# Two-block transformer kernel: the split weight buffers placed 128 bytes further on

## The chip, the cores and the metric

The kernel runs on one NeuronCore of a Trainium2 chip. The metric is the time of one execution on the device, in microseconds (us); of several runs the median counts.

## The reference

The input is 256 tokens of 1024 features, with 16 meta tokens put ahead, so T = 272. Two layers of a first block follow, and then one layer of a second block with attention, a gated scan and a mixture of experts. In the first block all matrix products are of this kind:

```python
for l in range(DEPTH):                                  # DEPTH = 2
    h = h + 0.5 * swiglu(rmsnorm(h, ffn1_norm[l]), ffn1_w_gate[l], ffn1_w_up[l], ffn1_w_down[l])   # d_ff 2816
    proj = rmsnorm(h, mix_norm[l]) @ w_in[l]            # 1024 x 3584
    ...                                                 # retention and differential attention
    h = h + jnp.concatenate([y_ret, y_diff], axis=-1) @ w_out[l]
    h = h + 0.5 * swiglu(rmsnorm(h, ffn2_norm[l]), ffn2_w_gate[l], ffn2_w_up[l], ffn2_w_down[l])
```

All of it is float32.

## The kernel before, in words

Features lie on the 128 partitions and tokens along the free dimension; h is 8 chunks of 128 features by 272 tokens. Weights stream from memory into a ring of 7 slots of 8 KB per partition; the queue that starts these DMAs is SyncE's, in an order written out as a list (FILLS). The ring tensor has 12 slots' length: behind the seven slots come four buffers, w_split0 to w_split3, of 8 KB per partition each, and a last stretch for small things (rv, rstd, lam_prod, mod_sums, and later in the second block ctx_acc, ctx_sq, f2eps, last_sum, S_acc).

A product in float32 is made from three matmuls in the faster type float32r. Each half slot of weights (1024 floats per partition, eight blocks of 128 x 128) is split: ScalarE writes the rounded part w_hi into a w_split buffer (`weights_hi`, L1517), then VectorE writes the rest w_lo = w - w_hi behind it (`weights_lo`, L1987). The activations are split in the same way, into x_hi and x_lo for the products that read h, hid_hi and hid_lo for the down projections, y_hi and y_lo for the output projection of the mixer. TensorE then adds w_hi x_hi + w_hi x_lo + w_lo x_hi in PSUM:

```python
pe.matmul(to, w[:, 0, k], hi, start=first, stop=False)      # L754
pe.matmul(to, w[:, 0, k], lo, start=False, stop=False)      # L755
return pe.matmul(to, w[:, 1, k], hi, start=False, stop=last_)   # L756
```

In each, the block w[:, i, k] (128 floats, 512 bytes per partition) is loaded as weights and hi or lo (272 columns, or 256 where the meta tokens are no longer wanted) is streamed. Semaphores pass the buffers on: split_ready counts VectorE's halves, split_used TensorE's, and ScalarE may overwrite a buffer four halves later. `ffn` runs through 22 pairs of gate and up tiles (x) and then 22 blocks of the down projection (hid) for each of four feed-forward stages, `mixer` through 28 input tiles (x) and 8 output tiles (y) in each layer.

Where these operands lie matters for what follows. In the built program the ring begins at byte 16,512 of each partition and the arena, which holds the activations, at byte 114,816. x_hi and x_lo begin at arena + 4 x 2224 and then every 1280 bytes, that is at byte 123,712 and on; hid_hi and hid_lo at byte 168,000 and on, every 1280 bytes; y_hi at 167,936 and y_lo at 176,640, every 1088 bytes without a gap. With 256 columns the x and y operands are read from 64 bytes further on, and the hid operands from their start. w_split0 begins at ring + 7 x 8192 = 73,856. The output projection of the second block (L1303, L1308, L1309) has weight buffers of its own in the ring's range, at multiples of 4096 from the ring's start, and streams y2_lo and y2_hi in chunks of 1024 bytes from bytes 131,712 and 139,904, both of them 128 past a multiple of 256.

Of the kernel before, what the change touches and what calls it, by code (L numbers as in the profile page):

```python
# [12 lines left out]
P = 128  # L13
D = 1024
C = D // P
META, SEQ = 16, 256
T = META + SEQ
DEPTH = 2
# [9 lines left out]
SLOT = 2048  # L28
NS = 7
SPLITS = 4  # L30
# [4 lines left out]
MOD_COLS = SLOT // C  # L35
# [21 lines left out]
MOD_BUFFERS = 3  # L57
# [175 lines left out]
def build(nc, stream_ffn, stream_in, stream_out, stream_mod, stream_in2, stream_out2, stream_expert,  # L233
# [4 lines left out]
    with ExitStack() as ctx:  # L238
        def sb(name, shape, dt=fp32):
            return ctx.enter_context(nc.sbuf_tensor(name, shape, dt))  # L240
# [5 lines left out]
        ring = sb("ring", [P, 12 * SLOT])  # L246
        ring_at = nc.sbuf_base - 4 * 12 * SLOT
# [8 lines left out]
        def cut(tensor, at, *shape):  # L256

            n = int(np.prod(shape))
            piece = tensor[:, at:at + n]
            if len(shape) == 1:  # L260
                return piece
            names = "abcd"[:len(shape)]
            sizes = dict(zip(names[1:], shape[1:]))
            return piece.rearrange(f"p ({' '.join(names)}) -> p {' '.join(names)}", **sizes)

        def layout(tensor, at, items):

            found = {}
            for name, *shape in items:
                found[name] = cut(tensor, at, *shape)  # L270
                at += int(np.prod(shape))
            assert at <= tensor.shape[1], (at, tensor.shape)
            return found
# [12 lines left out]
        def parts(name, byte, *shape):  # L286

            n = int(np.prod(shape))
            return cut(nc.alloc_sbuf_tensor_at(name, [P, n], f32r, offset=byte), 0, *shape)
# [6 lines left out]
        def spaced(name, at, n):  # L296

            return [parts(f"{name}{c}", arena_at + 4 * (at + c * STEP), T) for c in range(n)]

        x_hi, x_lo = spaced("x_hi", C * T + LEAD, C), spaced("x_lo", C * T + LEAD + C * STEP, C)  # L300
        w_split = [parts(f"w_split{b}", ring_at + 4 * (NS + b) * SLOT, 2, C, P) for b in range(SPLITS)]
        X_AT = (NS + SPLITS) * SLOT
        m = layout(ring, X_AT, [("rv", 3, 512), ("rstd", T)])
        rv, rstd = m["rv"], m["rstd"]
        lam_prod = cut(ring, X_AT, DEPTH * 2, 64)

        hid = cut(arena, rest, F, T)
        gate_act = cut(con, CON["axial_cos"][0], 4, T)
# [5 lines left out]
        m = layout(arena, rest, [("tables", 4, T), ("cos", 2, T), ("swap", 2, T), ("vT", 2, T), ("e", 2, 2, T), ("rot", 8, T)])  # L314
# [6 lines left out]
        m = layout(arena, rest + 38 * T, [("dv", 3, 512), ("aT", 2, 3, P), ("first", 2, P), ("sT", DEC)])  # L321
# [4 lines left out]
        m = layout(small, 0, [("lam", DEPTH * 4), ("lam_dot", DEPTH * 2), ("neglam", DEPTH), ("sub", DEPTH)])  # L326
        lam_dot, neglam, sub_w = m["lam_dot"], m["neglam"], m["sub"]
        m = layout(small, 736, [("max", 2, 2), ("negmax", 2, 2), ("rsum", 2), ("nr", 2), ("sum", 9, 2), ("ss", 9), ("bn", 2, 6), ("mv", 9, 2),
                                ("dev", 18), ("ms", 2, META)])
# [26 lines left out]
        m = layout(arena, C * T, [("z", 4, KEYS), ("k", 4, KEYS), ("state", 4, 64), ("t1", 4, KEYS), ("B", 4, SEQ), ("G", 4, SEQ),  # L356
                                  ("q", 2, SEQ)])
# [4 lines left out]
        m = layout(arena, at_sq, [("zv", 4, SEQ), ("kdT", 8, P)])  # L362
        zv, kdT = m["zv"], m["kdT"]
        m = layout(arena, at_std, [("u", SEQ), ("s", SEQ), ("qx", 4, SEQ), ("vtok", 4, P)])
# [5 lines left out]
        m = layout(ring, NS * SLOT, [("qraw", 4, SEQ), ("qsin", 4, SEQ), ("qcos", 4, SEQ), ("qsq", 4, SEQ), ("kraw", KEYS), ("ksq", KEYS),  # L370
                                     ("kstd", KEYS), ("kcos", SEQ), ("ksin", SEQ), ("lev", 2, 4 * SEQ)])
# [3 lines left out]
        v_sq = q_sq.rearrange("p a b -> p (a b)")[:, 0:512].rearrange("p (h d) -> p h d", d=64)  # L375
        m = layout(ring, X_AT, [("S", 8, P), ("va", 2, SEQ), ("mix", 2, 2, P)])
        S_acc, mlp_v, mlp_mix = m["S"], m["va"], m["mix"]
        m = layout(ring, X_AT, [("acc", SEQ), ("one_sq", SEQ), ("f2", C, P)])
        ctx_acc, ctx_sq, f2eps = m["acc"], m["one_sq"], m["f2"]
        last_sum = cut(ring, X_AT + 2 * SEQ + C * P, SEQ)  # L380
        sh2b = cut(con, CON["ret_cos"][0], C, P)
        S_cross = cut(con, CON["ret_cos"][0], 2, 2, 2, P)
        m = layout(con, CON["decay"][0], [("wr", C, GROUPS + E), ("u", 2, SEQ), ("g", 2, SEQ)])
        w_r, mlp_u, hg = m["wr"], m["u"], m["g"]
        m = layout(arena, at_t1, [("oh", 2, SEQ), ("ohsq", 2, SEQ), ("ohstd", 2 * SEQ)])
# [11 lines left out]
        m = layout(arena, at_ex + 2 * D, [("xs", C, P), ("act", FE), ("hid", FE), ("hidT", 4, P), ("sel", 2, 2, CAP), ("selg", 2, 2, CAP),  # L397
                                          ("turned", SEQ), ("zeros", SEQ)])
# [7 lines left out]
        m = layout(arena, at_R, [  # L406
            ("lg", 2, GROUPS + E), ("gmax", 2), ("ngmax", 2), ("gsum", 2), ("gexp", 2, GROUPS), ("t4", 2, GROUPS),
            ("i4", 2), ("one4", 2, GROUPS), ("em", 2, GROUPS, PER_GROUP), ("m1", 2, GROUPS), ("m2", 2, GROUPS), ("dm", 2, GROUPS),
            ("t32", 2, GROUPS, PER_GROUP), ("i32", 2, GROUPS), ("allowed", 2, GROUPS, PER_GROUP), ("oh1", 2, E), ("oh2", 2, E),
            ("d", 2), ("ex", 2), ("g1", 2), ("g2", 2), ("gate", 2, E), ("chosen", 2, E), ("never", 2, E), ("total", E),  # L410
            ("rank", 2, E), ("most", 1), ("slot_gate", 1)])
# [9 lines left out]
        m = layout(more, 0, [("cr", SEQ), ("fa", C), ("f2", C), ("qstd", 16), ("rqs", 16), ("nrq", 16), ("amax", AHEAD, 2), ("anm", AHEAD, 2),  # L421
                             ("asum", AHEAD, 2), ("ars", AHEAD, 2), ("std3", 4), ("wr2", C, GROUPS + E), ("brow", GROUPS + E), ("zero", 80)])
        ctx_r, fa, f2, q_std, rqs, nrq = (m[x] for x in ("cr", "fa", "f2", "qstd", "rqs", "nrq"))
# [4 lines left out]
        m = layout(small, MOD_AT, [("mod", 48, 2), ("a1", C, 2), ("a2", C), ("cc", C, 2), ("unit", 64), ("ss", 8), ("vstd", 8), ("vr", 8),])  # L428
        mod_row = cut(arena, ARENA - P, P)
        mod, a1, a2, cc, unit_row, v_ss, v_std, v_rstd = (m[x] for x in ("mod", "a1", "a2", "cc", "unit", "ss", "vstd", "vr"))  # L430
        mod_product = cut(arena, hid_end, C, MOD_COLS)
        mod_sums = cut(ring, X_AT, MOD_BUFFERS, 2, MOD_COLS)
        assert hid_end + SLOT <= ARENA - P and MOD_BUFFERS * 2 * MOD_COLS <= 3 * 512
        SH1, SC1, G1, SH2, SC2, G2 = (slice(C * i, C * i + C) for i in range(6))

# [2574 lines left out]
```

## Time and profile before

| | us |
|---|---|
| median of 3 runs | 1729.33 (1729.3 to 1729.35) |
| the profiled execution, its own time | 1730.19 |
| its span, first to last instruction | 1728.6 |
| matmuls busy | 1700.6 |
| weight loads busy | 1394.3 |
| VectorE busy | 979.4 |
| ScalarE busy | 796.9 |
| GpSimd busy | 168.5 |

Matmuls overlap each other in the pipeline, so a matmul's duration in the profile is longer than the time that it adds; the step from the start of one to the start of the next is what it adds. Weight loads (PEld) run beside the matmul before them. The first block's work ends at about 1085 us; the experts fill the time from about 1270 us to the end.

### The profile page before, as it was taken

The page shows a single profiled execution, that of the slowest core. Times are in us where ns is not written, and L with a number is a line of the kernel's source. Part 1 is how long each engine was busy: PE and PEld are TensorE (multiplying, and loading weights), DVE is VectorE, ACT ScalarE, POOL GpSimd, SP SyncE. Part 2 cuts the span into 40 slices and gives each one's busy share as a digit, 9 for nine tenths or more (in the row PEclk, how much of TensorE's full clock was granted, in tenths as well). Part 3 has the DMA queues.
Part 4 walks back from the last instruction along what each step waited for, and adds up shares of the span by engine and source line. Part 5 has one row for each costly group of instructions (what it writes and reads, how often), then busy time and mean ns, then how long its engine had stood idle before and what let it go on. Part 6 is the DMA issues. An engine that isn't in the chain of part 4 may idle for free.

```text
span 1728.6 us, 30190 instructions
## 1 busy us (share of the span) xinstructions
PE 1700.6 (98%) x12315; PEld 1394.3 (81%) x12316; DVE 979.4 (57%) x1689; ACT 796.9 (46%) x1432; POOL 168.5 (10%) x173
## 2 busy tenths in 40 slices
PE   8999999999999999999999999999999999999998
PEld 7999988999999999998999999678764544445443
DVE  6776577678767777678778666476621111121111
ACT  6664455466656765665455445455621111111111
POOL 1000053210000100014413000101410000000000
PEclk9999999999999999999999999999999999999999
DMA  9555552254576577574245456032399999999997
GB/s 371 196 214 225 171 168 102 98 173 161 228 270 243 198 265 268 207 233 140 105 161 216 171 192 201 32 83 74 143 419 402 430 427 427 428 428 429 428 427 302
DMA packets 79107, 425.88 MB, mean 246 GB/s; under 512 B 16385, under 2 KB 33025, under 8 KB 42113
## 3 DMA queue, kind: packets, MB, share of 16 engines
q1 hardware_dynamic: 78400, 421.80, 63.2%
q8 instruction: 89, 1.46, 0.3%
q10 hardware_dynamic: 576, 2.29, 0.3%
q14 instruction: 42, 0.34, 0.1%
HBM read 423.02 MB, written 1.05 MB: 245 GB/s over the span
## 4 chain that ended last, share of the span: by engine, by line
PE 82%; DMA 6%; DVE 5%; ACT 4%; issue 1%; DVEq 1%; POOL 0%; POOLq 0%; SPq 0%; ACTq 0%
PE ps L754 16%; PE ps L755 16%; PE ps L756 16%; PE ps L1404 10%; DMA ring<-stream_expert 5%; PE ps L1455 5%; PE ps L1378 3%; PE ps L1083 2%; PE ps L1077 2%; DVE w_split L1987 2%; ACT w_split L1517 2%; PE ps L1089 2%; PE ps L1385 1%; PE ps L1386 1%; DVEq L2112 1%
## 5 line engine op out<-in xcount | busy, mean ns | idle before, releaser
L1987 DVE TENSOR_TENSOR w_split<-ring,w_split 128x1024 fp32r<-128x1024 f32 x335 | 421.7, 1279 | 239.5 <-ACT w_split L1517 238.9
L754 PE MATMUL ps<-x_hi,w_split 128*128 128x272 f32 (+1 forms) x1856 | 539.8, 291 | 6.5 <-DVE arena L2183 2.4
L755 PE MATMUL ps<-x_lo,w_split 128*128 128x272 f32 (+1 forms) x1856 | 530.9, 286 | 0.0
L756 PE MATMUL ps<-x_hi,w_split 128*128 128x272 f32 (+1 forms) x1856 | 530.8, 286 | 0.0
L1517 ACT ACTIVATE w_split<-ring 128x1024 fp32r<-128x1024 f32 x335 | 344.7, 1051 | 220.0 <-PE ps L756 218.6
L754 PEld LDWEIGHTS ps<-x_hi,w_split 128*128 128x128 f32 x1856 | 351.8, 190 | 14.6 <-issue 5.8
L755 PEld LDWEIGHTS ps<-x_lo,w_split 128*128 128x128 f32 x1856 | 351.9, 190 | 0.2
L756 PEld LDWEIGHTS ps<-x_hi,w_split 128*128 128x128 f32 x1856 | 351.7, 189 | 0.0
L754 PE MATMUL ps<-hid_hi,w_split 128*128 128x272 f32 (+1 forms) x704 | 200.0, 284 | 0.8 <-DVE arena L2106 0.8
L755 PE MATMUL ps<-hid_lo,w_split 128*128 128x272 f32 (+1 forms) x704 | 199.9, 284 | 0.0
L756 PE MATMUL ps<-hid_hi,w_split 128*128 128x272 f32 (+1 forms) x704 | 199.8, 284 | 0.0
L1404 PE MATMUL ps<-ring,arena 128*64 128x512 f32 x704 | 187.4, 594 | 3.8 <-DMA ring<-stream_expert 3.1
L1404 PEld LDWEIGHTS ps<-ring,arena 128*64 128x64 f32 x704 | 58.6, 137 | 99.5 <-issue 94.5
L2737 DVE TENSOR_TENSOR arena<-arena,ps 128x512 f32<-128x512 f32 x16 | 11.0, 688 | 217.6 <-PE ps L1404 217.6
L754 PEld LDWEIGHTS ps<-hid_hi,w_split 128*128 128x128 f32 x704 | 132.5, 188 | 1.1 <-DVE arena L2106 1.1
L755 PEld LDWEIGHTS ps<-hid_lo,w_split 128*128 128x128 f32 x704 | 132.5, 188 | 0.0
L756 PEld LDWEIGHTS ps<-hid_hi,w_split 128*128 128x128 f32 x704 | 132.5, 188 | 0.0
L1606 ACT ACTIVATE con<-con 128x272 f32<-128x272 f32 (+1 forms) x88 | 37.7, 428 | 157.1 <-DVE con L2104 156.2
L1914 ACT ACTIVATE arena<-ps,small 128x128 f32<-128x128 f32 x64 | 24.1, 456 | 163.3 <-PE ps L1378 163.3
L1594 ACT ACTIVATE ring<-ring,small 128x256 f32<-128x256 f32 x192 | 81.3, 494 | 0.0
L1455 PE MATMUL ps<-ring,arena 128*64 128x512 f32 x352 | 78.1, 595 | 0.0
L2748 DVE SCALAR_TENSOR_TENSOR ye_lo<-ps,arena,ye_hi 128x512 fp32r<-128x512 f32 x32 | 24.0, 751 | 91.5 <-ACT ye_hi L1930 76.6
(438 smaller groups left out, 2362.9 us busy)
## 6 DMA issues: line engine op xcount, KB each, us to landing
ring<-stream_ffn SPq DMA_DIRECT2D x131, 1024.0 KB, 4.9
ring<-stream_expert SPq DMA_DIRECT2D x48, 2048.0 KB, 24.9
ring<-stream_expert SPq DMA_DIRECT2D x36, 1024.0 KB, 12.4
arena<-stream_expert SPq DMA_DIRECT2D x16, 2048.0 KB, 25.4
ring<-stream_in SPq DMA_DIRECT2D x27, 1024.0 KB, 4.8
ring<-stream_mod SPq DMA_DIRECT2D x24, 1024.0 KB, 5.0
con<-stream_expert SPq DMA_DIRECT2D x8, 2048.0 KB, 26.1
ring<-stream_out SPq DMA_DIRECT2D x12, 1024.0 KB, 4.8
```

The source lines that it names most:

```text
L754: pe.matmul(to, w[:, 0, k], hi, start=first, stop=False)
L755: pe.matmul(to, w[:, 0, k], lo, start=False, stop=False)
L756: return pe.matmul(to, w[:, 1, k], hi, start=False, stop=last_)
L1077: last = pe.matmul(ps[:, b, 0:KEYS], w[:, c], x2n[:, :, c], start=c == 0, stop=c == C - 1)
L1083: last = pe.matmul(ps[:, b, i * SEQ:i * SEQ + SEQ], w[:, i, c], x2n[:, 0, c], start=c == 0, stop=c == C - 1)
L1378: last = pe.matmul(ps[:, 6 + half, (c % 4) * P:(c % 4) * P + P], h2t[:, t, c * P:c * P + P], sel[:, t], start=t == 0, stop=t == 1)
L1404: last = pe.matmul(ps[rows, 4 + part, 0:FE], xs[:, c, rows], w, start=c == 0, stop=c == C - 1)
L1455: last = pe.matmul(ps[rows, 6 + half, 0:512], hidT[:, f, rows], w[:, half * 512:half * 512 + 512], start=f == 0, stop=f == FE // P - 1)
L1517: nc.scalar.activation(w_split[n % SPLITS][:, 0], half_of(n), ACT.Copy).then_inc(hi_ready, 1)
L1594: last = nc.scalar.activation(to[:, c], w[:, c], ACT.Identity, scale=cc[:, c, v:v + 1])
L1606: nc.scalar.activation(gate_act[:, j % 4, t:T], gate_act[:, j % 4, t:T], ACT.Silu).then_inc(gate_act_ready, 1)
L1987: nc.vector.tensor_tensor(w[:, 1], half_of(n), w[:, 0].bitcast(fp32), ALU.subtract).then_inc(split_ready, 1)
```

## The change

The four w_split buffers begin 32 floats (128 bytes) further on, and so do most of the things that lie behind them. Nothing else is touched: the ring's slots, the activations, and every instruction, wait and DMA stay.

```diff
-        w_split = [parts(f"w_split{b}", ring_at + 4 * (NS + b) * SLOT, 2, C, P) for b in range(SPLITS)]
+        W_AT = NS * SLOT + 32
+        w_split = [parts(f"w_split{b}", ring_at + 4 * (W_AT + b * SLOT), 2, C, P) for b in range(SPLITS)]
         X_AT = (NS + SPLITS) * SLOT
-        m = layout(ring, X_AT, [("rv", 3, 512), ("rstd", T)])
+        FIRST_X = X_AT + 32
+        m = layout(ring, FIRST_X, [("rv", 3, 512), ("rstd", T)])
         rv, rstd = m["rv"], m["rstd"]
-        lam_prod = cut(ring, X_AT, DEPTH * 2, 64)
+        lam_prod = cut(ring, FIRST_X, DEPTH * 2, 64)
...
-        m = layout(ring, X_AT, [("acc", SEQ), ("one_sq", SEQ), ("f2", C, P)])
+        m = layout(ring, FIRST_X, [("acc", SEQ), ("one_sq", SEQ), ("f2", C, P)])
         ctx_acc, ctx_sq, f2eps = m["acc"], m["one_sq"], m["f2"]
-        last_sum = cut(ring, X_AT + 2 * SEQ + C * P, SEQ)
+        last_sum = cut(ring, FIRST_X + 2 * SEQ + C * P, SEQ)
...
-        mod_sums = cut(ring, X_AT, MOD_BUFFERS, 2, MOD_COLS)
+        mod_sums = cut(ring, FIRST_X, MOD_BUFFERS, 2, MOD_COLS)
```

## Rows read from the trace of the kernel before

**Rows 1.** The page's sections 1 and 4, and the granted clock by core.
```profile
PE 1700.6 (98%) x12315; PEld 1394.3 (81%) x12316; DVE 979.4 (57%) x1689; ACT 796.9 (46%) x1432; POOL 168.5 (10%) x173
...
PE ps L754 16%; PE ps L755 16%; PE ps L756 16%; PE ps L1404 10%; DMA ring<-stream_expert 5%; PE ps L1455 5%; PE ps L1378 3%; PE ps L1083 2%; PE ps L1077 2%; DVE w_split L1987 2%; ACT w_split L1517 2%; PE ps L1089 2%; PE ps L1385 1%; PE ps L1386 1%; DVEq L2112 1%
...
core 0: 1728.6 us, clock 0.998
```

**Rows 2.** Groups of TensorE by form: count | busy us, mean ns | idle before.
```profile
L754 PE MATMUL ps<-x_hi,w_split 128*128 128x272 f32 x1416 | 413.8, 292 | 6.1 <-DVE arena L2183 2.4 <-DVE x_lo L1992 2.2 <-DVE w_split L1987 1.4
...
L754 PE MATMUL ps<-hid_hi,w_split 128*128 128x272 f32 x528 | 151.4, 287 | 0.8 <-DVE arena L2106 0.8
...
L754 PE MATMUL ps<-x_hi,w_split 128*128 128x256 f32 x440 | 126.0, 286 | 0.4 <-ACT more L1602 0.2
...
L754 PE MATMUL ps<-hid_hi,w_split 128*128 128x256 f32 x176 | 48.6, 276 | 0.0
```

**Rows 3.** Timeline of TensorE, first and last of four stretches: start, duration, instruction.
```profile
574.84 0.29 PE L756 MATMUL ps<-x_hi,w_split 128*128 128x272 f32 x1
...
586.92 0.29 PE L755 MATMUL ps<-x_lo,w_split 128*128 128x272 f32 x1
...
699.78 0.29 PE L755 MATMUL ps<-hid_lo,w_split 128*128 128x272 f32 x1
...
711.99 0.28 PE L755 MATMUL ps<-hid_lo,w_split 128*128 128x272 f32 x1
...
914.80 0.28 PE L754 MATMUL ps<-x_hi,w_split 128*128 128x256 f32 x1
...
926.92 0.28 PE L756 MATMUL ps<-x_hi,w_split 128*128 128x256 f32 x1
...
1039.79 0.28 PE L754 MATMUL ps<-hid_hi,w_split 128*128 128x256 f32 x1
...
1051.91 0.28 PE L756 MATMUL ps<-hid_hi,w_split 128*128 128x256 f32 x1
```

**Rows 4.** Timeline, output projection of the second block: two rows, 22 steps apart.
```profile
1250.61 0.28 PE L1309 MATMUL ps<-y_lo,o_hi 128*128 128x256 f32 x1
...
1253.25 0.28 PE L1303 MATMUL ps<-y_hi,o_lo 128*128 128x256 f32 x1
```

**Rows 5.** Timeline, projection of y, one output tile: L754 of each chunk.
```profile
351.38 0.29 PE L754 MATMUL ps<-y_hi,w_split 128*128 128x272 f32 x1
...
351.76 0.29 PE L754 MATMUL ps<-y_hi,w_split 128*128 128x272 f32 x1
...
352.14 0.29 PE L754 MATMUL ps<-y_hi,w_split 128*128 128x272 f32 x1
...
352.52 0.29 PE L754 MATMUL ps<-y_hi,w_split 128*128 128x272 f32 x1
...
352.90 0.29 PE L754 MATMUL ps<-y_hi,w_split 128*128 128x272 f32 x1
...
353.28 0.29 PE L754 MATMUL ps<-y_hi,w_split 128*128 128x272 f32 x1
...
353.65 0.29 PE L754 MATMUL ps<-y_hi,w_split 128*128 128x272 f32 x1
...
354.04 0.29 PE L754 MATMUL ps<-y_hi,w_split 128*128 128x272 f32 x1
...
354.41 0.29 PE L754 MATMUL ps<-y_hi,w_split 128*128 128x272 f32 x1
```

**Rows 6.** Timeline, projection of y with 256 columns, 86 steps apart.
```profile
884.75 0.28 PE L755 MATMUL ps<-y_lo,w_split 128*128 128x256 f32 x1
...
894.89 0.28 PE L754 MATMUL ps<-y_hi,w_split 128*128 128x256 f32 x1
```

**Rows 7.** The filling instructions by line: count, duration ns min/median/max, starts, form.
```profile
L1987 DVE TENSOR_TENSOR w_split<-ring,w_split x335: 1211/1226/1814, 12.9 to 1075.5; 128x1024 fp32r<-128x1024 f32 x168
...
L1517 ACT ACTIVATE w_split<-ring x335: 1038/1047/1064, 11.8 to 1074.4; 128x1024 fp32r<-128x1024 f32 x168
```

## The prediction

> **What bounds the kernel now.** I read the page first: TensorE's matmuls are busy for 1700.6 us of a span of 1728.6 us [rows 1], so only something that shortens or lengthens the row of matmuls itself can move the time much. The chain that ended last says the same, and says where: the three lines of the split product (L754, L755, L756) hold 48% of the span, while the two instructions that fill the moved buffers (L1987 on VectorE, L1517 on ScalarE) hold 2% each [rows 1]. The groups by form then give the number of these products: 1416 x 3 = 4248 matmuls of 272 columns on x, 528 x 3 = 1584 of 272 columns on hid, 440 x 3 = 1320 of 256 columns on x and 176 x 3 = 528 of 256 columns on hid [rows 2] (of each three rows the first stands there); the rest, 384, work on y. The granted clock is 0.998 over the span [rows 1], that is, the upper level of 2.4 GHz, so the clock is not what limits them.
>
> The duration of one matmul (286 ns) is not what one costs, since they overlap. What one costs is the step from start to start, and I took it from the timeline, from the first and last of about a hundred in a stretch without a gap:
> - x, 272 columns: (586.92 - 574.84) / 98 = 123.3 ns [rows 3]
> - hid, 272 columns: (711.99 - 699.78) / 99 = 123.3 ns [rows 3]
> - x, 256 columns: (926.92 - 914.80) / 101 = 120.0 ns [rows 3]
> - hid, 256 columns: (1051.91 - 1039.79) / 107 = 113.3 ns [rows 3]
>
> The reader is to see the last two: same instruction form, same engine, same clock, same weight buffers, and 6.7 ns apart. Even the best is above its columns (256 / 2.4 = 106.7 ns; 272 / 2.4 = 113.3 ns). What differs between the two is where the operand that streams lies. So place in memory has a price in this kernel, and a change of place can be worth something in either direction. 7680 matmuls lie in these four groups, 0.45 ns on each of them is 3.5 us, or 0.2%.
>
> **The addresses.** From the layout in the code, with the ring at byte 16,512: a weight block begins at 73,856 + 512 i, which is 128 past a multiple of 256; after the change at 73,984 + 512 i. That is a multiple of 256, and by my sum 256 past a multiple of 512, not on one. Whether the period that matters is 256 or 512 the trace has to say; I will call the byte modulo 256 the phase. x_hi and x_lo have phase 64 for 272 columns and 128 for 256 columns (they start 16 floats later), hid_hi and hid_lo always 64. I call "distance" the phase of the streamed operand less that of the weights. Before: x and hid at 272 columns 192, x at 256 columns 0, hid at 256 columns 192. After, each less 128: 64, 128 and 64. The output projection of the second block has both operands at phase 128, thus distance 0 with other buffers, and its step is (1253.25 - 1250.61) / 22 = 120.0 ns [rows 4], the same as x at 256 columns: that speaks for the distance (or the pair of phases) as what sets the step.
>
> The best witness for the distances that come is the projection of y: its chunks are 1088 bytes long, so the eight chunks go through all four phases under an unchanged weight phase. In the order c = 4, 5, 6, 7, 0, 1, 2, 3 the starts of L754 are 0.38, 0.38, 0.38, 0.38, 0.38, 0.37, 0.39 and 0.37 us apart [rows 5]. By distance that is, per matmul: 128 (c = 4, 0) 126.7 ns; 192 (c = 5, 1) 125.0 ns; 0 (c = 6, 2) 128.3 ns; 64 (c = 7, 3) 125.0 ns. The rows are rounded to 0.01 us, so each of these is good to some 1.5 ns. Two distances that differ by 128 cost the same within that, and the odd ones cost less than the even ones. The change adds exactly 128. The witness has a weakness: its phases change every three matmuls, and it does not settle. At distance 192 it gives 125.0 ns where the steady stream gives 123.3, and with 256 columns its mean is (894.89 - 884.75) / 86 = 117.9 ns [rows 6], between the steady 120.0 and 113.3.
>
> **The change, part by part.**
> 1. x and hid at 272 columns, 5832 matmuls, distance 192 to 64. Not shown steady. Lower bound: the best step per column in the trace, 113.3 / 256 x 272 = 120.4 ns, so -2.9 x 5832 = -17 us. Upper bound: the worst of the y rows, 128.3 ns, so +5.0 x 5832 = +29 us. The nearest row is y's at distance 64, which equals y's at 192; I take 0.
> 2. x at 256 columns, 1320 matmuls, distance 0 to 128. Lower bound: 113.3 ns, -6.7 x 1320 = -8.8 us. Upper bound: above 120.0 no steady row of this width lies; y's difference of 192 to 0 (3.3 ns) once more on top would be +4.4 us. I take the mean of y at this width, 117.9: -2.1 x 1320 = -2.8 us.
> 3. hid at 256 columns, 528 matmuls, distance 192 to 64. From 0 (stays at 113.3) to +6.7 x 528 = +3.5 us (goes to 120.0). I take the same 117.9: +4.6 x 528 = +2.4 us.
> 4. y, 384 matmuls: the same four distances, dealt to other chunks: 0, within 384 x 1 ns = 0.4 us.
> 5. L1517 and L1987, 335 each. They write the moved buffer, and L1987 reads it beside the ring, which does not move. L1517 takes 1047 ns (1038 to 1064), L1987 1226 ns with a longest of 1814 ns [rows 7]. That two VectorE instructions of one shape differ so shows that something can hold them up, but TensorE's idle time before the 272-column products of x that ends on L1987 is 1.4 us in all [rows 2], and their cover is the ring of four buffers. If the cover went, it would be the 4% of the span that the chain gives them: 5% more on each is 0.04 x 1728.6 x 0.05 = 3.5 us. Only a longer run of such stalls counts. I take 0.
> 6. The things behind the buffers (rv, rstd, the context sums, f2eps, mod_sums) move by the same 128 bytes. They hold no instruction of the chain's larger lines; no instruction, wait or DMA is added or removed anywhere, the DMAs write the ring's seven slots, which stay, and the queues keep their order. 0.
>
> Sum: 0 - 2.8 + 2.4 + 0 = -0.4 us against the profiled execution's 1730.19 us (span 1728.6 us). The median of the runs is 1729.33 us, 0.86 us below the profiled one, and the forecast is made against it: 1729.33 - 0.4 = 1729 us, no change that this kernel's measurement tells (0.2% is 3.5 us).
>
> The Trainium skill speaks to this on its page "TensorE: Matmul & The Clock Gate", in "Step-by-step: what each phase is for": TensorE has two independent read ports, and loading the next weights takes no bandwidth from the running matmul. By that rule no distance could matter and the time stays; by the rows above a distance matters by up to 6.7 ns, so the measurement decides, and the rule adds no weight to the forecast. The page's isolated gap ("Back-to-back issue gap", columns / 2.4 + 2.5 ns) would be 115.8 and 109.2 ns; the trace has 123.3, 120.0 and 113.3.
>
> **The rivals.**
> - Faster, x at 256 columns leaves its bad place. Distance 0 is the one case where both operands start in the same phase, and it is the slowest steady row. If 128 is as good as 192: 113.3 ns, -8.8 us, 1720.5 us. For it: the 6.7 ns are there. Against: y at distance 128 (126.7) is nearer to 0 (128.3) than to 192 (125.0).
> - Faster, all 272-column products gain. If what costs is that a weight block lies 128 off its natural border, and not the distance, then 5832 matmuls come down towards 120.4 ns: 1729.3 - 17 = 1712 us, half of it 1721 us. Against: hid at 256 columns runs at 113.3 with the weights where they are.
> - Slower, the other side: distance 64 is a worse steady place than 192 for 272 columns. It decides from 0.6 ns per matmul on (0.6 x 5832 = 3.5 us). At y's 125.0 ns it is +1.7 x 5832 = +10 us, 1739 us; at 128.3 it is 1758 us. For it: 123.3 is already below every y row, so the present place may be a lucky one that the move loses. Against: y's equal 125.0 at 192 and 64.
> - Slower, hid at 256 columns alone loses its 113.3: +3.5 us, 1732.8 us, on the border of what can be told.
> - The change does nothing, since the cost repeats every 128 bytes, or since no phase of the weights matters: 1729.3 us. It cannot be told from the forecast by the time, only by the steps; it shares the forecast's chance. By my address sum the blocks reach a multiple of 256 only, so if what counts were the border of 512, the change would also miss it.
>
> **How the numbers follow.** Chances: no change (forecast and "does nothing") 0.38; x at 256 columns gains 0.23; all 272 columns gain 0.13; 272 columns lose 0.17; hid at 256 alone loses 0.06; VectorE and ScalarE slow down so that it shows 0.03. Faster by over 0.2%: 0.23 + 0.13 = 0.36. Slower: 0.17 + half of 0.06 + 0.03 = 0.23. Within: 0.38 + half of 0.06 = 0.41. The likeliest case's own range is 1726 to 1733 us. For 8 in 10, the range goes down past the x case (1720.5) to 1718 and up to y's 125.0 (1739); outside lie most of the 272-column gain and the deep end of the loss.
>
> **What would show it.** The steps from start to start in the same four stretches: I expect 123 to 124 ns at 272 columns for x and hid, 113 to 120 for x at 256 columns and 113 to 120 for hid at 256. In y's rows the pairs should change places by chunk and the mean stay at 126 and 118 ns. L1987 and L1517 should keep 1226 and 1047 ns. I am wrong if the steady step at 272 columns moves by more than 0.6 ns, in whichever direction; that one number decides.

## The result, and the profile after

The changed kernel takes 1745.03 us in the median of 4 runs (1744.63 to 1745.87), before 1729.34 us (1729.3 to 1733.19). The ratio is 1.009, with a 95% interval of 1.0078 to 1.0101: slower by 15.7 us. The profiled execution took 1744.85 us, with a span of 1743.2 us, 14.6 us more than before.

The page of the changed kernel, its sections 1 and 4 (all line numbers are two higher than before):

```profile
PE 1717.2 (99%) x12315; PEld 1411.1 (81%) x12316; DVE 978.1 (56%) x1689; ACT 797.9 (46%) x1432; POOL 169.4 (10%) x173
...
PE 88%; DMA 6%; DVE 3%; ACT 2%; issue 1%; DVEq 0%; SPq 0%; POOL 0%; POOLq 0%; ACTq 0%
PE ps L756 18%; PE ps L758 18%; PE ps L757 18%; PE ps L1406 10%; DMA ring<-stream_expert 5%; PE ps L1457 5%; PE ps L1380 3%; PE ps L1085 2%; PE ps L1079 2%; PE ps L1091 2%; DVE w_split L1989 1%; ACT w_split L1519 1%; PE ps L1387 1%; PE ps L1388 1%; PE ps L934 0%
```

Matmuls are busy for 1717.2 us, 16.6 us more, and the number of instructions is the same [rows 1]. The chain now has the three product lines at 54% where they had 48%, and the two filling lines L1989 and L1519 have fallen from 2% to 1% each; all of VectorE and ScalarE hold 3% and 2% of it, where they held 5% and 4%. So the loss is in TensorE's own row, and the waits for the other engines became smaller.

The timeline of the changed kernel in the four kinds of stretch that the prediction used, first and last matmul of each:

```profile
579.75 0.29 PE L757 MATMUL ps<-x_lo,w_split 128*128 128x272 f32 x1
...
591.91 0.29 PE L757 MATMUL ps<-x_lo,w_split 128*128 128x272 f32 x1
...
709.77 0.29 PE L758 MATMUL ps<-hid_hi,w_split 128*128 128x272 f32 x1
...
721.93 0.29 PE L758 MATMUL ps<-hid_hi,w_split 128*128 128x272 f32 x1
...
929.78 0.28 PE L758 MATMUL ps<-x_hi,w_split 128*128 128x256 f32 x1
...
941.88 0.28 PE L758 MATMUL ps<-x_hi,w_split 128*128 128x256 f32 x1
...
1049.77 0.28 PE L757 MATMUL ps<-hid_lo,w_split 128*128 128x256 f32 x1
...
1061.90 0.28 PE L758 MATMUL ps<-hid_hi,w_split 128*128 128x256 f32 x1
```

From start to start that is (591.91 - 579.75) / 96 = 126.7 ns for x and (721.93 - 709.77) / 96 = 126.7 ns for hid at 272 columns, where it was 123.3 [rows 3]; (941.88 - 929.78) / 102 = 118.6 ns for x at 256 columns (120.0 before); and (1061.90 - 1049.77) / 103 = 117.8 ns for hid at 256 columns (113.3 before). The sum over the matmuls: 3.4 x 5832 = 19.8 us, -1.4 x 1320 = -1.8 us, 4.5 x 528 = 2.4 us, together 20.4 us. The span grew by 14.6 us, so 5.8 us of this did not reach the time.

Both traces, read whole, say where it went. From the first to the last start of each group, with the waits in it, the time grew by 9.4 us for x and 4.2 us for hid at 272 columns and by 2.3 us for hid at 256. It fell by 1.4 us for x at 256 and stayed for y. Together this is 14.4 us.

- Waits, 3.9 us. From 20 us on, steps of 140 ns and more from one product to the next, with whatever lies between, were 174 before, 110.4 us in all, and 165 after, 105.4 us; the nine that went cost 1.1 us as ordinary steps. This is no accident of one trace: the two experiments below with the distances of the changed kernel show 105.4 us each, and the six that keep those of the kernel before in most of their rows show 108.9 to 111.0 us (the one that adds instructions left out). It fits with a slower TensorE that finds its operands ready more often.
- The start, 0.9 us. Between 9 and 12 us and between 12 and 14 us, among the first products and their waits, the granted clock was 0.72 and 0.57 in the trace before, and 1.00 in the one after. An experiment with the changed kernel's distances has slow steps there too, so this does not come from the change.
- The last 1 us is the rounding of the steps, and the mixers' rows at 272 columns, which do not settle and moved by less than 3.4 ns.

The groups by form of the changed kernel show one place where a wait went:

```profile
L756 PE MATMUL ps<-x_hi,w_split 128*128 128x272 f32 x1416 | 415.9, 294 | 6.3 <-DVE arena L2185 2.2 <-DVE x_lo L1994 1.9 <-DVE w_split L1989 1.9
...
L756 PE MATMUL ps<-hid_hi,w_split 128*128 128x272 f32 x528 | 152.6, 289 | 0.0
```

The idle time ahead of hid's products, 0.8 us before [rows 2], is gone. Ahead of x's it is the same. What this view calls idle is only a part; steps that stretch while the engine still counts as busy are the rest.

The instructions that fill the moved buffers, by line, and one stretch of y in the changed kernel:

```profile
L1989 DVE TENSOR_TENSOR w_split<-ring,w_split x335: 1211/1225/1795, 12.5 to 1089.9; 128x1024 fp32r<-128x1024 f32 x168
...
L1519 ACT ACTIVATE w_split<-ring x335: 1039/1056/1065, 11.5 to 1088.8; 128x1024 fp32r<-128x1024 f32 x168
```

```profile
349.71 0.29 PE L757 MATMUL ps<-y_lo,w_split 128*128 128x272 f32 x1
...
360.93 0.29 PE L756 MATMUL ps<-y_hi,w_split 128*128 128x272 f32 x1
```

L1989 has 1225 ns in the median and L1519 1056 ns, against 1226 and 1047 [rows 7]. The 9 ns of L1519 are not the price of the place: with the weights moved and the row at its old pace (the first experiment below) it takes 1048 ns, and with the weights where they were and the row slow (the second) 1057 ns. The mean step of y is (360.93 - 349.71) / 89 = 126.1 ns, as before.

### The profile page after: what moved, and what is told of

It is laid out like the page before. It is cut to its first block, busy times and chain, and to the rows that moved or that the text cites. A ratio compares the mean times of both kernels' runs of the same rounds, so it can differ in the third digit from the quotient of the medians.

```text
span 1743.2 us, 30190 instructions
## 1 busy us (share of the span) xinstructions
PE 1717.2 (99%) x12315; PEld 1411.1 (81%) x12316; DVE 978.1 (56%) x1689; ACT 797.9 (46%) x1432; POOL 169.4 (10%) x173
## 4 chain that ended last, share of the span: by engine, by line
PE 88%; DMA 6%; DVE 3%; ACT 2%; issue 1%; DVEq 0%; SPq 0%; POOL 0%; POOLq 0%; ACTq 0%
PE ps L756 18%; PE ps L758 18%; PE ps L757 18%; PE ps L1406 10%; DMA ring<-stream_expert 5%; PE ps L1457 5%; PE ps L1380 3%; PE ps L1085 2%; PE ps L1079 2%; PE ps L1091 2%; DVE w_split L1989 1%; ACT w_split L1519 1%; PE ps L1387 1%; PE ps L1388 1%; PE ps L934 0%
## 5 line engine op out<-in xcount | busy, mean ns | idle before, releaser
L1989 DVE TENSOR_TENSOR w_split<-ring,w_split 128x1024 fp32r<-128x1024 f32 x335 | 420.7, 1275 | 254.8 <-ACT w_split L1519 254.4
L1519 ACT ACTIVATE w_split<-ring 128x1024 fp32r<-128x1024 f32 x335 | 345.6, 1052 | 240.5 <-PE ps L758 238.5
```

What stands on the lines that cost most here:

```text
L1519: nc.scalar.activation(w_split[n % SPLITS][:, 0], half_of(n), ACT.Copy).then_inc(hi_ready, 1)
L1989: nc.vector.tensor_tensor(w[:, 1], half_of(n), w[:, 0].bitcast(fp32), ALU.subtract).then_inc(split_ready, 1)
```

## The experiments

Everything below is read in the same way: the step from start to start in a stretch of about a hundred matmuls. The kernel before ran beside the experiments on the same chips, at 1729.77 us in the median for the first four, 1729.64 us for the next four and 1729.5 us for the last three. Five of the kernels ran once only (the two shifts of the weights, the small things, the two sweeps); their steps carry the argument. Distances are in bytes modulo 256, streamed operand less weights.

**Is it the distance, or the place of the weights?** Two kernels make a square of the two. In the first, weights and operands both move (LEAD was 48):

```diff
-        w_split = [parts(f"w_split{b}", ring_at + 4 * (NS + b) * SLOT, 2, C, P) for b in range(SPLITS)]
+        W_AT = NS * SLOT + 32
+        w_split = [parts(f"w_split{b}", ring_at + 4 * (W_AT + b * SLOT), 2, C, P) for b in range(SPLITS)]
...
-        x_hi, x_lo = spaced("x_hi", C * T + LEAD, C), spaced("x_lo", C * T + LEAD + C * STEP, C)
+        X_LEAD = 16
+        x_hi, x_lo = spaced("x_hi", C * T + X_LEAD, C), spaced("x_lo", C * T + X_LEAD + C * STEP, C)
...
+        H_AT = hid_at + 32
```

> The weight buffers lie 128 bytes further on, as in the change, and x and hid lie 128 bytes further on too (for x the start is 128 bytes back, which is the same phase modulo 256). So the weights have phase 0 and the distances are those of the kernel before: 192 at 272 columns, 0 for x at 256, 192 for hid at 256. Theory of the distance: steps of 123.3, 120.0 and 113.3 ns and 1729 us (within 3 us; y keeps the changed distances). Theory of the weights' own phase: 126.7, 118.7 and 117.8 ns as in the changed kernel, and 1745 us.

1729.55 us, ratio to before 0.9999 (0.999 to 1.0009). Its timeline, three of the stretches (x at 272, x at 256, hid at 256):

```profile
579.83 0.28 PE L759 MATMUL ps<-x_lo,w_split 128*128 128x272 f32 x1
...
591.91 0.28 PE L758 MATMUL ps<-x_hi,w_split 128*128 128x272 f32 x1
...
929.74 0.28 PE L760 MATMUL ps<-x_hi,w_split 128*128 128x256 f32 x1
...
941.98 0.28 PE L760 MATMUL ps<-x_hi,w_split 128*128 128x256 f32 x1
...
1049.75 0.28 PE L759 MATMUL ps<-hid_lo,w_split 128*128 128x256 f32 x1
...
1061.99 0.28 PE L759 MATMUL ps<-hid_lo,w_split 128*128 128x256 f32 x1
```

12.08 / 98 = 123.3 ns, 12.24 / 102 = 120.0 ns, 12.24 / 108 = 113.3 ns. The weights lie where the change put them, and the loss is gone.

The mirror leaves the weights and moves x and hid alone (the last two edits of the diff above without the first).

> The mirror: the weight buffers stay where they were (phase 128), and x and hid move by 128 modulo 256. The distances are those of the changed kernel: 64, 128, 64. Theory of the distance: steps of 126.7 (272 columns), 118.7 (x, 256) and 117.8 ns (hid, 256), and 1744 to 1745 us. Theory of the weights' own phase: 123.3, 120.0 and 113.3 ns, and 1729 us. If only x's and hid's own phase counts, the result is a third set, equal to that of the kernel with both moved.

1745.55 us, ratio 1.0092 (1.0075 to 1.0109). Its timeline, x at 272 and hid at 256 columns:

```profile
579.82 0.29 PE L757 MATMUL ps<-x_lo,w_split 128*128 128x272 f32 x1
...
591.98 0.29 PE L757 MATMUL ps<-x_lo,w_split 128*128 128x272 f32 x1
...
1049.81 0.28 PE L757 MATMUL ps<-hid_lo,w_split 128*128 128x256 f32 x1
...
1061.94 0.28 PE L758 MATMUL ps<-hid_hi,w_split 128*128 128x256 f32 x1
```

12.16 / 96 = 126.7 ns and 12.13 / 103 = 117.8 ns: the whole loss, with the weights untouched. The weights' own place has no price; their distance to the streamed operand has. One number missed the expectation, x at 256 columns:

```profile
929.72 0.28 PE L757 MATMUL ps<-x_lo,w_split 128*128 128x256 f32 x1
...
941.96 0.28 PE L757 MATMUL ps<-x_lo,w_split 128*128 128x256 f32 x1
```

12.24 / 102 = 120.0 ns where 118.7 was expected. The row was at 118.6 ns before an interruption near 922 us and again after one near 992 us; the changed kernel had 118.6 to 118.7 ns in the same stage but for one half slot, with 120.0. More on this below.

**Is it 256 or 512, and did the change do what it says?** The blocks of the changed kernel begin on an odd multiple of 256. With 96 floats in the place of 32 they begin on a multiple of 512 (byte 74,240), and with 64 floats they lie 256 bytes further on than before.

> The weight buffers lie 384 bytes further on, so that a block begins on a real multiple of 512 (byte 74,240); modulo 256 that is the same phase as in the changed kernel. If the pattern repeats every 256 bytes: 126.7, 118.7, 117.8 ns and 1744 to 1746 us, as the changed kernel. If the border of 512 is what counts: steps at 272 columns of 123.3 ns or less, and 1729 us or less.

> The weight buffers lie 256 bytes further on, the same phase modulo 256 as before. If the pattern repeats every 256 bytes: 123.3, 120.0 and 113.3 ns and 1729 to 1730 us. If it repeats every 512 bytes: other steps in at least one of the four groups.

The first took 1745.84 us, the second 1729.65 us. One stretch of x at 272 columns in each, first the one on the border of 512, then the one 256 bytes on:

```profile
579.75 0.29 PE L757 MATMUL ps<-x_lo,w_split 128*128 128x272 f32 x1
...
591.91 0.29 PE L757 MATMUL ps<-x_lo,w_split 128*128 128x272 f32 x1
```

```profile
579.83 0.29 PE L757 MATMUL ps<-x_lo,w_split 128*128 128x272 f32 x1
...
591.92 0.29 PE L756 MATMUL ps<-x_hi,w_split 128*128 128x272 f32 x1
```

126.7 ns and 12.09 / 98 = 123.4 ns. In these rows the pattern repeats every 256 bytes, and a block that really begins at a multiple of 512 loses just as much. The other stretches are those of the changed kernel and of the kernel before, but for x at 256 columns in the first of the two, which has both 120.0 and 118.6 ns, like the mirror.

**The small things behind the buffers.** FIRST_X = X_AT + 32 alone, with w_split where it was.

> The other half of the change alone: rv, rstd, lam_prod, mod_sums and the context sums lie 128 bytes further on, the weight buffers stay. Theory of the distance: nothing but 1729 to 1730 us, and steps of 123.3, 120.0 and 113.3 ns. Rival (part of the loss comes from these, for instance from the factors that VectorE reads at every eviction): over 1732 us.

1729.72 us, with steps of 123.3, 123.3, 120.0 and 113.3 ns. They cost nothing.

**The map of distances.** x may lie 0 to 48 floats behind its region's start, and each stage may have a start of its own; so two kernels measure all distances in steps of 32 bytes.

```diff
-        x_hi, x_lo = spaced("x_hi", C * T + LEAD, C), spaced("x_lo", C * T + LEAD + C * STEP, C)
+        X_LEAD = [0, 8, 24, 32, 40, 0]
+        X = [(spaced(f"x{i}_hi", C * T + a, C), spaced(f"x{i}_lo", C * T + a + C * STEP, C)) for i, a in enumerate(X_LEAD)]
...
+        H_MORE = [8, 24, -8, 16]
```

X_LEAD has one start for each stage in order (feed-forward, mixer, feed-forward, feed-forward, mixer, feed-forward), H_MORE one shift of hid for each feed-forward stage.

> Weights as before, x at another distance in each stage: 0, 32, 96 and 128 at 272 columns, then 160 (272 columns) and 224 (256 columns) in the second mixer, 64 at 256 columns in the last stage; hid at 224, 32, 160 (272 columns) and 0 (256 columns). Theory of the distance: x at 64 and 256 columns takes hid's 117.8 ns, hid at 0 and 256 columns takes x's 120.0 ns; at 272 columns 0 and 128 lie above 123.3 ns, near 127. Multiples of 32 between are unknown; if the pattern is one of 64-byte pieces they lie between their neighbours. Rival (each operand has a price of its own): x and hid differ at the same distance.

> The rest of the distances: x at 160, 64, 192 and 96 at 272 columns in the first four stages, 96 (272) and 160 (256) in the second mixer, 96 at 256 columns in the last stage; hid at 128, 96, 64 (272 columns) and 32 (256 columns). Theory of the distance: x and hid at 64 take 126.7 ns, x at 192 takes 123.3 ns, and where the sweep before had hid at a distance, x takes the same here (160 at 272 columns). Rival as there.

They took 1739.08 and 1740.73 us, the second with X_LEAD = [40, 16, 48, 24, 24, 8] and H_MORE = [-16, 40, 32, 24]. Of the first sweep, hid at 160 (272 columns), x at 64 and hid at 0 (256 columns):

```profile
704.82 0.29 PE L757 MATMUL ps<-hid_hi,w_split 128*128 128x272 f32 x1
...
716.90 0.29 PE L759 MATMUL ps<-hid_hi,w_split 128*128 128x272 f32 x1
...
999.83 0.28 PE L759 MATMUL ps<-x_hi,w_split 128*128 128x256 f32 x1
...
1011.97 0.28 PE L757 MATMUL ps<-x_hi,w_split 128*128 128x256 f32 x1
...
1049.77 0.28 PE L757 MATMUL ps<-hid_hi,w_split 128*128 128x256 f32 x1
...
1061.89 0.28 PE L759 MATMUL ps<-hid_hi,w_split 128*128 128x256 f32 x1
```

12.08 / 98 = 123.3 ns, 12.14 / 103 = 117.9 ns and 12.12 / 101 = 120.0 ns. x takes what hid had at 64 (117.8 ns), and hid takes what x had at 0: they have no price of their own. Of the second, x at 160 and hid at 128, both 272 columns:

```profile
44.80 0.29 PE L757 MATMUL ps<-x_hi,w_split 128*128 128x272 f32 x1
...
56.88 0.29 PE L759 MATMUL ps<-x_hi,w_split 128*128 128x272 f32 x1
...
149.77 0.29 PE L757 MATMUL ps<-hid_hi,w_split 128*128 128x272 f32 x1
...
161.93 0.29 PE L757 MATMUL ps<-hid_hi,w_split 128*128 128x272 f32 x1
```

12.08 / 98 = 123.3 ns and 12.16 / 96 = 126.7 ns. All together, in ns per matmul:

| distance | 0 | 32 | 64 | 96 | 128 | 160 | 192 | 224 |
|---|---|---|---|---|---|---|---|---|
| 272 columns | 125.3 | 125.6 to 125.7 | 126.7 | 125.3 or 126.7 | 126.7 | 123.3 | 123.3 or 126.7 | 125.3 |
| 256 columns | 120.0 | 117.8 | 117.8 | 120.0 | 118.6 or 120.0 | 117.4 | 113.3 or 117.8 | 118.3 |

(160 and 224 at 256 columns are from two further runs below. Where two numbers stand with "or", both came, in different stretches; at 192 and 272 columns nearly all stretches had 123.3. The weights lay 0 or 128 past a multiple of 256 in all runs.) The kernel before lay at 192 in three of its four groups, the best place at either width. Of the eight places, only its neighbour 160 is as good at 272 columns.

**Using the map.** If x at 256 columns lies at 0, the worst place, moving it alone should pay. X_LEAD = [48, 48, 48, 48, 48, 32] puts it at 192 in the last feed-forward stage; everything else stays as before.

> Kernel before, with one edit: in the last feed-forward stage alone (1056 matmuls of 256 columns on x) x_hi and x_lo lie 64 bytes further back, so that their distance to the weights is 192 instead of 0. Theory of the distance: the step there falls from 120.0 to the 113.3 ns that hid has at 192, 6.7 x 1056 = 7.0 us less; some of it may come back as waits, so 1722 to 1724 us. Rival (hid's 113.3 ns has another cause than the distance, for instance its tiles or its order): the step stays at 120 ns and the time at 1729.5 us.

1726.08 us in the median of 12 runs, from 1722.52 to 1729.81, ratio 0.998 (0.9971 to 0.999). This is faster than both kernels, but it is above the 1722 to 1724 us expected, 3.6 us gained instead of 7.0, and it scatters. The profiled execution took 1725.62 us, and its timeline shows a reason. Three stretches of the same stage, same instruction, same addresses, and one row between them:

```profile
897.74 0.28 PE L756 MATMUL ps<-x_hi,w_split 128*128 128x256 f32 x1
...
904.99 0.28 PE L757 MATMUL ps<-x_lo,w_split 128*128 128x256 f32 x1
...
907.87 0.70 PE L752 MATMUL ps<-arena,con 128*128 128x272 f32 x2 [1.13 <-POOL arena L2808]
...
919.84 0.28 PE L757 MATMUL ps<-x_lo,w_split 128*128 128x256 f32 x1
...
931.97 0.28 PE L758 MATMUL ps<-x_hi,w_split 128*128 128x256 f32 x1
...
984.83 0.28 PE L756 MATMUL ps<-x_hi,w_split 128*128 128x256 f32 x1
...
996.96 0.28 PE L758 MATMUL ps<-x_hi,w_split 128*128 128x256 f32 x1
```

The first goes at 7.25 / 64 = 113.3 ns, the second at 12.13 / 103 = 117.8 ns, the third at 12.13 / 107 = 113.4 ns. The granted clock is 1.00 in all three. Between the first and the second TensorE waited 1.13 us for GpSimd's sum (L752). Between the second and the third it was interrupted twice: near 976 us, after which it stayed at 117.8 ns, and at 979.94 us, where it had been idle for 0.27 us, and after which it went at 113.3 ns. So one distance can have two levels, and the row keeps the one on which it was last started; an interruption can change the level and need not. In all kept traces no stretch of x or hid changes its level between two interruptions. The kernel with both moved shows the same at 272 columns, in its first stage:

```profile
44.77 0.29 PE L760 MATMUL ps<-x_hi,w_split 128*128 128x272 f32 x1
...
56.93 0.29 PE L760 MATMUL ps<-x_hi,w_split 128*128 128x272 f32 x1
...
109.73 0.29 PE L760 MATMUL ps<-x_hi,w_split 128*128 128x272 f32 x1
...
121.94 0.29 PE L760 MATMUL ps<-x_hi,w_split 128*128 128x272 f32 x1
```

12.16 / 96 = 126.7 ns, and after an interruption at about 80 us 12.21 / 99 = 123.3 ns, both at distance 192. The two numbers at 128 (118.6 and 120.0 ns at 256 columns, in the mirror) and at 96 (125.3 and 126.7 ns at 272) are of this kind too. At distance 64 and 272 columns every settled stretch had 126.7 ns, which is also the upper level of 192; whether a distance sets a price or only which levels are open was not tested.

**Other distances for that stage.**

> As the run with x moved in the last feed-forward stage, but to distance 160 instead of 192 (256 columns, 1056 matmuls). At 272 columns 160 and 192 gave the same 123.3 ns. Theory of the distance with two locked levels: steps at one of the two levels that 192 has shown at 256 columns, 113.3 or 117.8 ns, so 1722 to 1727 us; if 160 holds the lower level throughout, 1722 to 1723 us. Rival (160 is as bad as 0 at this width): 120.0 ns and 1729.5 us.

> The same with distance 224 in the last stage; the second mixer's x at 160 (272 columns) and 224 (256 columns, 264 matmuls). At 272 columns 224 gave 125.3 ns, between the 123.3 of 192 and the 126.7 of others. Theory of the distance: a step at 256 columns between 113.3 and 120.0 ns, and 1723 to 1728 us. Rival: 120.0 ns and 1729 to 1730 us.

1729.1 us, ratio 0.9997 (0.9988 to 1.0007), with a step of 117.4 ns; and 1728.86 us, ratio 0.9996 (0.9986 to 1.0006), with 118.3 ns. Both times missed what was expected (1722 to 1727 and 1723 to 1728 us), and 117.4 ns is neither of the two levels of 192. The second kernel also moves x in the second mixer, to 160 and 224. Both keep one level through the stage. Each saves some 2 ns on 1056 matmuls and cannot be told from before. In the second, hid at 256 columns, which was not touched and lies at 192, shows the other level too:

```profile
1049.79 0.28 PE L756 MATMUL ps<-hid_hi,w_split 128*128 128x256 f32 x1
...
1061.92 0.28 PE L757 MATMUL ps<-hid_lo,w_split 128*128 128x256 f32 x1
```

12.13 / 103 = 117.8 ns, where the kernel before had 113.3 [rows 3]. This was the slowest of its ten executions, 1732.35 us, and 4.5 x 528 = 2.4 us of that is hid's level.

**Starting the row alike each time.**

```diff
                 w = split_half(n)
+                if now[0] == 5:
+                    pe.matmul(ps[:, bank, 496:512], ident16, causal16[:, 0:16], start=True, stop=True)
```

> As the run with x at distance 192 in the last feed-forward stage, and one more small matmul (16 columns, bf16, into columns that nothing reads) ahead of each half of weights in that stage, 42 in all. It breaks the even row of steps at the same place each time. If the two levels (113.3 and 117.8 ns at one distance) are set by how the row was last started, every half now starts alike, and all of them take one level: all 113.3 ns (1722 to 1723 us in every run) or all 117.8 ns (1727 to 1728 us in every run), and the runs scatter less than the 7.3 us between the lowest and the highest of that kernel. Rival (the levels come from something outside this row, such as what VectorE, ScalarE or the DMAs do at the time): both levels go on side by side and the runs scatter as before.

1734.17 us, from 1733.23 to 1735.96, ratio 1.0026 (1.0016 to 1.0037). The scatter falls from 7.3 to 2.7 us. In the profiled execution 41 of the 42 restarted halves run at the upper level, 117.8 ns, and one, near the start of the stage, at 113.4 ns; the first two halves, which have no restart, had the lower level too. One of the restarts:

```profile
931.88 0.28 PE L758 MATMUL ps<-x_hi,w_split 128*128 128x256 f32 x1
932.00 0.18 PE L790 MATMUL ps<-con 128*128 128x16 bf16 x1
932.04 0.36 PE L756 MATMUL ps<-x_hi,w_split 128*128 128x256 f32 x1
932.24 0.28 PE L757 MATMUL ps<-x_lo,w_split 128*128 128x256 f32 x1
```

From the product ahead of it to the second behind it are 0.36 us, where two ordinary steps take 0.24. With 42 of them that is some 5 us, and hid behind them runs at 117.8 ns (+2.4 us), against -2.3 us for x: the kernel loses, and its time is 6 us above the higher of the two that I expected. I had expected all halves on one level. The rival, that the levels come from outside the row, would have left both side by side; 41 of 42 speak for the start of the row. The one exception shows that the small matmul alone does not fix the level.

## Why the prediction was wrong

- **What bounds it: right.** The loss is in TensorE's row of products, and a quantity of a few ns on each of 5832 matmuls is the whole result.
- **That distance is what counts, modulo 256: right.** The square of two experiments and the shift by 256 bytes show it. That the blocks come to a multiple of 256 and not of 512 was right too, and makes no difference.
- **Item 1, "the nearest row is y's at distance 64, which equals y's at 192; I take 0": this failed.** It measured +3.4 ns, 19.8 us, within the bounds of -17 and +29 us that I gave and then kept out of the range. Of these 19.8 us, 13.5 us reached the time. y's chunks change their distance every three matmuls, and their steps belong to a row that never settles; in a settled row 192 gives 123.3 and 64 gives 126.7 ns. I had written down that weakness, that y at 192 showed 125.0 ns where the settled row has 123.3, and did not draw the conclusion: a witness that is wrong by 1.7 ns at the one distance that can be checked cannot show a difference of 0 at another. The rounding of the rows to 0.01 us was not at fault. Over all eight tiles of y at 272 columns the trace before gives 124.8 ns at 192 and 124.9 at 64, 126.9 at 128 and 126.6 at 0, so the reading was right for y. But in the changed kernel y's own chunks at 192 take 125.8 ns, those at 64 take 125.2, those at 0 125.8: in such a row the step is not set by the chunk's own distance. In settled rows at 272 columns the pairs 128 apart differ: 32 and 160 (125.6 and 123.3 ns), 64 and 192.
- **Item 2, x at 256 columns, -2.8 us: right in sign, -1.8 us.** Item 3, hid at 256 columns, +2.4 us: right, +2.4 us. That the mean of y was near the truth here is luck: y's steps at this width lie within 117.9 to 118.4 ns at all four distances, the settled ones between 113.3 and 120.0.
- **Items 4 to 6, 0: right.** y's mean stayed at 126.1 ns, L1989 kept its time and L1519's 9 ns more cost nothing, and the small things cost nothing in a run of their own.
- **A term that was missing:** waits. A slower row of products gave back 3.9 of the 20.4 us in shorter waits. No term of the sum stood for this.
- **The rivals.** "Distance 64 is a worse steady place than 192" is what happened, and its test (0.6 ns per matmul) decided as said; its reason, that 123.3 was below every y row and the present place perhaps a lucky one, was the right one to weigh more. Its chance was 0.17, and its two prices, 1739 and 1758 us, stand on both sides of the 1745 us measured; the range ended at the lower one, y's 125.0 ns, which is the same unsettled witness.
- **The Trainium skill's page "TensorE: Matmul & The Clock Gate"** says in "Step-by-step: what each phase is for" that loading the next weights takes no read bandwidth from the running matmul. The runs here differ: with nothing changed but the distance of the two operands, the step goes from 113.3 to 120.0 ns at 256 columns. What happens inside, whether the two reads meet in the same part of the buffer, was not measured by itself and stays open, and so does what selects the level at a restart.

## What to carry to other kernels

When matmuls follow each other without a gap, measure the step from start to start and not the duration, for each pair of operands, and compare groups of one form: a difference between them can be a price of place, as here, or of a level on which the row was started. Moving one operand to a rounder address is not an improvement by itself; what counted here was the distance between the weights and the streamed operand modulo 256, and the map of it was made by a sweep in which each stage had a start of its own. Before a row of a trace serves as witness for a case that is not in it, check it where both are known, and let its error there set the range.

## What the runs showed of the hardware

- At 2.4 GHz, with a granted clock of 0.997 to 0.999, a float32r matmul with 128 columns of weights costs 123.3 to 126.7 ns at 272 columns and 113.3 to 120.0 ns at 256, by the distance of its operands and, at some distances, by the level of the row.
- At one distance (192) a row can run at two levels, 113.3 or 117.8 ns (256 columns) and 123.3 or 126.7 ns (272 columns); 128 at 256 columns (118.6 or 120.0 ns) and 96 at 272 (125.3 or 126.7 ns) showed two as well. It keeps its level for hundreds of matmuls and changed it in these traces only where the row was interrupted. By estimate the two levels of x and hid in the last stage are worth 4.5 x (1056 + 528) = 7.1 us; the last-stage kernel, a constant program, scattered over 7.3 us (1722.5 to 1729.8 us). Only one of its twelve executions has a trace, so that this is the cause of the scatter is not shown.
